# Retention in 64-token blocks packed into parts of the tensor array, and a gate product in four column groups

## The reference

```
def _retention_chunk(R, q, k, v):            # one block of L = CHUNK = 64 tokens
    s = einsum(q, k) * decay                  # causal, gamma ** (i - j)
    inner = einsum(s, v)
    cross = einsum(q, R) * q_dec              # gamma ** (i + 1)
    R_new = gamma ** L * R + einsum(k * k_dec, v)
    return R_new, inner + cross
r_out = _head_norm(r_out) * silu(rg)          # mean and variance over the 128 values of a head
```

## Time and profile before

| | us |
|---|---|
| median of 3 runs | 1840.75 (1840.66 to 1842.19) |
| the profiled execution, its own time | 1841.68 |
| its span, first to last instruction | 1839.8 |
| PE busy in the span | 1793.3 (97%) |
| DVE busy | 1158.7 (63%) |
| ACT busy | 578.5 (31%) |
| POOL busy | 115.7 (6%) |
| mean granted clock of PE | 0.991 |

### The profile page before, as it was taken

How to read it: one execution, slowest core, us unless ns; L and a number is a source line. 1 busy time by engine, 2 the same in 40 slices (tenths; PEclk the granted TensorE clock), 3 DMA queues, 4 the chain that set the end, 5 groups by cost and what they waited for, 6 DMA issues and landing times.

```text
span 1839.8 us, 31050 instructions
## 1 busy us (share of the span) xinstructions
PE 1793.3 (97%) x9636; PEld 1481.0 (80%) x9636; DVE 1158.7 (63%) x2588; ACT 578.5 (31%) x2032; POOL 115.7 (6%) x278
## 2 busy tenths in 40 slices
PE   5999999999999999999799999999999999999997
PEld 3787888888888888888678888888888888888886
DVE  3665566655666555665666766766666666666666
ACT  3321222212222212222334434434434344344342
POOL 1000000000000000010000000000000000000000
PEclk8999999999999999999899999999999999999999
DMA  9665555555555555554765565575565665655655
GB/s 374 201 169 172 134 147 148 136 137 139 127 151 147 125 142 134 138 141 133 199 172 157 155 191 147 155 187 143 165 180 147 172 170 147 182 163 146 191 141 143
DMA packets 488465, 296.64 MB, mean 161 GB/s; under 512 B 348626, under 2 KB 423570, under 8 KB 487396
## 3 DMA queue, kind: packets, MB, share of 16 engines
q1 hardware_dynamic: 488420, 296.08, 58.6%
HBM read 174.27 MB, written 121.71 MB: 161 GB/s over the span
## 4 chain that ended last, share of the span: by engine, by line
PE 92%; DVE 2%; issue 2%; DMA 2%; ACT 1%; SPq 1%; POOL 0%; POOLq 0%; DVEq 0%; ACTq 0%
PE bank L1305 80%; PE bank L1478 3%; PE bank L1501 2%; PE bank L1403 2%; PE bank L1389 2%; PE bank L1395 2%; PE bank L1401 2%; PE bank L1508 1%; DVE wl L321 1%; DMA stage<-in_w_out 1%; DMA xn_scratch<-xn 0%; PE bank L1458 0%; SPq L517 0%; DMA aqk_row<-aqk_scratch 0%; DMA xt<-in_x_prompt 0%
## 5 line engine op out<-in xcount | busy, mean ns | idle before, releaser
L1305 PE MATMUL bank<-wh,hh 128*128 128x512 f32 x1584 | 397.9, 393 | 5.9 <-DVE hh L1085 2.7
L1305 PE MATMUL bank<-wh,hl 128*128 128x512 f32 x1584 | 392.7, 390 | 0.0
L1305 PE MATMUL bank<-wl,hh 128*128 128x512 f32 x1584 | 391.8, 389 | 0.5 <-DVE wl L321 0.5
L1305 PEld LDWEIGHTS bank<-wh,hl 128*128 128x128 f32 x1584 | 297.8, 188 | 61.9
L1305 PEld LDWEIGHTS bank<-wl,hh 128*128 128x128 f32 x1584 | 297.2, 188 | 62.7 <-DVE wl L321 0.9
L1305 PEld LDWEIGHTS bank<-wh,hh 128*128 128x128 f32 x1584 | 292.9, 189 | 66.9 <-issue 7.3
L726 ACT ACTIVATE hf<-xn,tiny_a 128x128 f32<-128x128 f32 (+1 forms) x248 | 98.6, 480 | 373.8 <-DVE xn L919 373.8
L1228 DVE SCALAR_TENSOR_TENSOR a_gate<-a_gate,bank 128x128 f32<-128x128 f32 x132 | 29.1, 282 | 175.1 <-ACT a_gate L875 175.1
L1305 PE MATMUL bank<-wh,yh 128*128 128x512 f32 x528 | 132.1, 392 | 0.0
L1305 PE MATMUL bank<-wh,yl 128*128 128x512 f32 x528 | 130.8, 389 | 0.0
L1305 PE MATMUL bank<-wl,yh 128*128 128x512 f32 x528 | 130.8, 389 | 0.0
(11 more groups left out here) (167 smaller groups left out, 2434.5 us busy)
## 6 DMA issues: line engine op xcount, KB each, us to landing
xt<-in_x_prompt SPq DMA_DIRECT2D x64, 512.0 KB, 3.9
p_scratch<-p_in SPq DMA_DIRECT2D x264, 96.0 KB, 1.8
p_in<-p_scratch SPq DMA_DIRECT2D x66, 384.0 KB, 3.5
h_scratch<-hf SPq DMA_DIRECT2D x33, 512.0 KB, 2.9
hf<-h_scratch SPq DMA_DIRECT2D x33, 512.0 KB, 4.8
out<-xt SPq DMA_DIRECT2D x32, 512.0 KB, 4.5
xn_scratch<-xn SPq DMA_DIRECT2D x31, 512.0 KB, 2.9
xp<-xn_scratch SPq DMA_DIRECT2D x124, 128.0 KB, 3.1
```

Source lines behind the costliest of these rows:

```text
L1305: ins = mm(out, a[:, k, :], b[:, k, :], start=first and n == part[0] and k == chunks[0], stop=last and n == part[-1] and k == chunks[-1])
```

## The change

Retention is worked in two blocks of 64 tokens within a tile of 128. With c the block and h the head:

- scores: for each head two matmuls, 128 rows and 64 columns of the array, 64 moving columns; the decay table and the product on DVE halve to 256 columns.
- state: two updates for each head, one for each block, 64 rows and 128 columns of the array, 128 moving columns, into two banks (`upd_b`, `ky_b`). DVE makes the state after the first block in a new tile `state_mid` (4 instructions, `mid_done`), and the state after the second from that.
- queries times state and scores times values move into `weighted_values`, which stands behind group 1 instead of ahead of it. It waits for `gn_done` of the slot before, `mid_done` and `st_done`. Queries times state: 8 matmuls, 128 rows and 64 columns, 128 moving columns. Scores times values: 8 matmuls of 64 rows and 64 columns, 128 moving columns, the four of two heads in four quarters of the array. Outputs lie in two banks (`out_b` for heads 0 and 2, `xb0` for heads 1 and 3); for the odd heads the two blocks lie in swapped halves, so that the head norm takes two DVE instructions for each of them.
- the residual gate's product goes in four column groups of 256 moving columns instead of two of 512; its rows, loads and stores go in four pieces.
- in slot 32 the transposes of k wait for `state_done`; slot 0 of phase B uses another bank and `weigh` waits once for `gn_done`.

```diff
         state_s = sb("state_s", [P, COLS], F32, phase_a)
+        state_mid = sb("state_mid", [P, COLS], F32, phase_a)
         r_gate = sb("r_gate", [P, COLS], F32, phase_a)
         r_out = sb("r_out", [P, COLS], F32, phase_a)
-        decay = sb("decay", [P, COLS], F32, phase_a)
+        decay = sb("decay", [P, RH * HALF], F32, phase_a)
...
+        def row_block(h, c):
+
+            return HALF * ((c + h) % 2)
+
+        def out_of(h):
+
+            return (out_b, xb0)[h % 2][:, h * DK:(h + 1) * DK]
...
                 if back:
                     wait(dve, s_ready, t)
                     wait(dve, out_ready, t - 1)
-                    V.tensor_tensor(s_t[:, :], qs_b[:, :], decay[:, :], ALU.mult).then_inc(st_done, 1)
+                    V.tensor_tensor(s_t[:, 0:RH * HALF], qs_b[:, 0:RH * HALF], decay[:, :], ALU.mult).then_inc(st_done, 1)
                 if front:
                     wait(dve, za_ready, 4 * t + 1)
                     wait(dve, rope_loaded, 16 * (t + 1))
                     wait(dve, q_turned, t)
                     wait(dve, k_done, t)
                     rotate(t, za0, q_row, zq_read, q_mul, q_done)
+                if back:
+                    wait(dve, upd_ready, t)
+                    wait(dve, out_ready, t - 1)
+                    wait(dve, state_done, t - 1)
+                    st = state_s if static(i) and t - 1 == SAMPLE else state
+                    for h in range(RH):
+                        cols = slice(h * DK, (h + 1) * DK)
+                        last = V.scalar_tensor_tensor(state_mid[:, cols], st[:, cols], GAMMA[h] ** HALF, upd_b[:, cols],
+                                                      ALU.mult, ALU.add)
+                    last.then_inc(mid_done, 1)
...
-                        last = V.bn_stats(gn_stats[:, h, :], out_b[:, h * DK:(h + 1) * DK])
+                        last = V.bn_stats(gn_stats[:, h, :], out_of(h))
...
-                    wait(dve, upd_ready, t)
-                    st = state_s if static(i) and t - 1 == SAMPLE else state
+                    wait(dve, mid_done, t)
                     for h in range(RH):
                         cols = slice(h * DK, (h + 1) * DK)
-                        last = V.scalar_tensor_tensor(st[:, cols], st[:, cols], GAMMA[h] ** P, upd_b[:, cols], ALU.mult, ALU.add)
+                        last = V.scalar_tensor_tensor(st[:, cols], state_mid[:, cols], GAMMA[h] ** HALF, ky_b[:, cols],
+                                                      ALU.mult, ALU.add)
                     last.then_inc(state_done, 1)
...
-                        last = V.tensor_scalar(r_out[:, cols], out_b[:, cols], gn_mv[:, h, 0:1], gn_rstd[:, h:h + 1],
-                                               ALU.subtract, ALU.mult)
+                        if row_block(h, 0) == 0:
+                            last = V.tensor_scalar(r_out[:, cols], out_of(h), gn_mv[:, h, 0:1], gn_rstd[:, h:h + 1],
+                                                   ALU.subtract, ALU.mult)
+                        else:
+                            for c in range(2):
+                                at = slice(row_block(h, c), row_block(h, c) + HALF)
+                                last = V.tensor_scalar(r_out[c * HALF:(c + 1) * HALF, cols], out_of(h)[at, :], gn_mv[at, h, 0:1],
+                                                       gn_rstd[at, h:h + 1], ALU.subtract, ALU.mult)
...
+            def weighted_values(i, t):
+
+                wait(pe, gn_done, t - 1)
+                wait(pe, mid_done, t)
+                st = state_s if static(i) and t - 1 == SAMPLE else state
+                for h in range(RH):
+                    for c in range(2):
+                        cols, at = slice(h * DK, (h + 1) * DK), row_block(h, c)
+                        if h == RH - 1 and c == 1:
+                            wait(pe, st_done, t)
+                        mm(out_of(h)[at:at + HALF, :], q_t[:, h * DK + c * HALF:h * DK + (c + 1) * HALF],
+                           (st, state_mid)[c][:, cols], start=h < 2, stop=False, tile_position=(0, at))
+                for h in range(RH):
+                    for c in range(2):
+                        rows, cols = slice(c * HALF, (c + 1) * HALF), slice(h * DK, (h + 1) * DK)
+                        at = row_block(h, c)
+                        last = mm(out_of(h)[at:at + HALF, :], s_t[rows, h * HALF:(h + 1) * HALF], v_row[rows, cols],
+                                  start=False, stop=h >= 2, tile_position=(c * HALF, at))
+                last.then_inc(out_ready, 1)
...
-                        c = slice(h * DK, (h + 1) * DK)
-                        last = mm(qs_b[:, c], k_t[:, c], q_t[:, c], start=True, stop=True)
+                        for c in range(2):
+                            tok = slice(h * DK + c * HALF, h * DK + (c + 1) * HALF)
+                            last = mm(qs_b[c * HALF:(c + 1) * HALF, h * HALF:(h + 1) * HALF], k_t[:, tok], q_t[:, tok],
+                                      start=True, stop=True, tile_position=(0, c * HALF))
                     last.then_inc(s_ready, 1)
                     wait(pe, state_done, t - 1)
                     wait(pe, v_done, t)
                     for h in range(RH):
-                        c = slice(h * DK, (h + 1) * DK)
-                        last = mm(upd_b[:, c], k_row[:, c], v_dec[:, c], start=True, stop=True)
+                        for c in range(2):
+                            rows, cols = slice(c * HALF, (c + 1) * HALF), slice(h * DK, (h + 1) * DK)
+                            last = mm((upd_b, ky_b)[c][:, cols], k_row[rows, cols], v_dec[rows, cols], start=True, stop=True,
+                                      tile_position=(c * HALF, 0))
                     last.then_inc(upd_ready, 1)
-                    wait(pe, gn_done, t - 1)
-                    st = state_s if static(i) and t - 1 == SAMPLE else state
-                    for h in range(RH):
-                        c = slice(h * DK, (h + 1) * DK)
-                        mm(out_b[:, c], q_t[:, c], st[:, c], start=True, stop=False)
-                        wait(pe, st_done, t)
-                        last = mm(out_b[:, c], s_t[:, c], v_row[:, c], start=False, stop=True)
-                    last.then_inc(out_ready, 1)
+                    if not front:
+                        weighted_values(i, t)
...
                         dense(za1[:, :], h_hi, h_lo, group(1)).then_inc(za_ready, 1)
+                    if back:
+                        weighted_values(i, t)
...
+                        wait(pe, state_done, t)
...
-                            for j in range(2):
-                                last = mm(xb0[32 * j:32 * j + 2, :], c_silu[:, 2 * s + kk, :],
-                                          stage_view(n)[:, kk, j * COLS:(j + 1) * COLS], start=s == 0 and kk == 0,
+                            for j in range(4):
+                                last = mm(qs_b[32 * j:32 * j + 2, KV:2 * KV], c_silu[:, 2 * s + kk, :],
+                                          stage_view(n)[:, kk, j * KV:(j + 1) * KV], start=s == 0 and kk == 0,
                                           stop=s == 3 and kk == 1, tile_position=(0, 32 * j))
...
+                if static(i) and t == 0:
+                    pe.wait_ge(gn_done, SAMPLE + 1)
...
-    causal = (p[:, None] <= p[None, :]).astype(np.float64)
+    causal = (p[:, None] <= q[None, :]).astype(np.float64)
```

More of the change, by code:

```diff
@@ L80, in build_program @@
         ident = sb("ident", [P, P])
-        small = sb("small", [P, 64])
+        small = sb("small", [P, 32])
         neg_half = small[:, 0:8]
@@ L119, in build_program @@
         gn_mv = tiny_a[:, 28:36].rearrange("p (h s) -> p h s", h=RH)
[L120 to L125, removed]
+        c_in = tiny_a[:, 4:20].rearrange("p (c k) -> p c k", c=2)
+        c_th = tiny_a[:, 20:36].rearrange("p (c k) -> p c k", c=2)
+        c_silu = tiny_a[:, 36:52].rearrange("p (k c) -> p k c", c=2)
+        g_col = tiny_a[:, 52:60]
+        h_scale = tiny_a[:, 60:76].rearrange("p (k c) -> p k c", c=2)
+        h_shift = tiny_a[:, 76:92].rearrange("p (k c) -> p k c", c=2)
         mod_rows = s_t
@@ L201, in build_program @@
             sem(n) for n in ("gn_stat_done", "gn_mv_done", "gn_var_done", "gn_rstd_done", "gn_done", "yr_done"))
-        state_out, wide_set = sem("state_out"), sem("wide_set")
+        state_out, wide_set, mid_done = sem("state_out"), sem("wide_set"), sem("mid_done")
         rows_cleared, h_front, hi_front, lo_front = sem("rows_cleared"), sem("h_front"), sem("hi_front"), sem("lo_front")
@@ L385, in ag_bank @@
         def ag_bank(i, t):
-            return out0_b if static(i) and t == 0 else kg_b
+            return out1_b if static(i) and t == 0 else kg_b
         def static(i):
             return isinstance(i, int)
+        def row_block(h, c):
+            return HALF * ((c + h) % 2)
+        def out_of(h):
+            return (out_b, xb0)[h % 2][:, h * DK:(h + 1) * DK]
         def pe_turns(i, t):
@@ L487, in slot @@
```

(25 more changed lines are left out.)

2 lines of the change are left out of this document (1 added, 1 removed).

## The result

The changed kernel takes 1986.3 us (median of 4 runs, 1985.32 to 1987.65) against 1840.7, a ratio of 1.0787 with a 95% interval of 1.0774 to 1.0801. It is slower, as forecast, but by 146 us where 69 were forecast, and outside the range. The span of the profiled execution is 1985.6 us against 1839.8, 145.8 more; mean granted clock 0.972 against 0.991.

What follows compares the result with a forecast made beforehand. PE, busy for all 635.00 us of phase A's body, bounds the kernel. Profiled 1841.68 + 71.7 for slots 1 to 32 - 2.5 for the rest = 1910.9, 0.93 above the median, so 1910; range 1884 to 1945.

Steps and rivals of the forecast that it cites:

- gate and slot 33: Residual gate's product some 3.5 us shorter, once; slot 33 about 1 us longer through waits and head norm; together -2.5.
- The new wait: Before group 3 in every slot, PE stalls 2.22 us for DVE's read of k, which stands behind `out_ready`.
- Two instructions more at 0.34: DVE's head norm gets two more instructions, half the partitions taking the same time: 2 x 0.34 = 0.68 us.
- rival 2: The clock falls in PE's stall, one slow piece of 1.2 us in each slot: 39 us, 1949; chance 0.09.
- Nothing gained on PE: Retention on PE comes to 3.51 us a slot against 3.49, six changes of the array's division costing 0.84.
- The steps' sum: Retention's packed matmuls on PE, counted in steps without changes of the array's division, take 2.67 us a slot.
- Issue rate: PE's issue of the scores: 16 records in 0.45 us, 0.028 each, should be possible; 0.89 is their bound.
- Rival 3: `v_row`'s loop at group 0 binds too, practically a tie; 0.4 us a slot gives 1923; chance 0.15, inside the forecast.
- The cover for `state_mid`: DVE's 3.3 us from scores to statistics, `state_mid` included, hide under PE's 6.6 us through group 1; cost nothing.

Runs made afterwards that it cites:

- filling experiment: Changed kernel plus 18 wide matmuls of unused result ahead of group 3's wait for k's rotation, from tile 6 on: 1958.92 us, ratio 1.0635 to the kernel before.
- addresses-back kernel: Changed kernel with `tiny_a` allocated ahead of `stage23` and a pad in phase B, so stationary tiles start at multiples of 256 bytes again: 1967.99 us, ratio 1.0689.
- k first with addresses: Changed kernel with DVE's rotation of k ahead of its wait for `out_ready`, and stationary tiles back at multiples of 256 bytes: 1884.09 us, ratio 1.0227.

## Why the prediction was right and wrong

The sign, the mechanism and its place were right; the size was not. The 145.8 us between the spans come apart like this:

| | forecast | measured | from |
|---|---|---|---|
| PE waits for k's read | 32 x 2.22 = 71 | 88: 80.2 recorded, 32 x 0.29 for ends and restarts, less 1.5 for the one wait before | waits of the profile, starts in the timeline |
| lower clock behind the waits | 0 | 37 | 23 pieces at 1.6 us, the filling experiment |
| addresses of stationary tiles | not named | 15 | phase B, slots of the addresses-back kernel |
| PE's own work | 32 x 0.02 = 1 | 6 | slot of k first with addresses, 25.56 against 25.35 |
| gate and slot 33 | -2.5 | about 0, by the remainder only | |

- **The new wait**, the step that decided: shown. Putting k's rotation first takes 91 us away, putting the block back and `state_mid` forward 90. The term was mis-sized: 2.22 forecast, some 2.7 measured from start to start (8.34 - 5.58 = 2.76 in the slot shown), and a restart behind it. "Two instructions more at 0.34" failed: all six follow each other at 0.43, 2.58 instead of 2.04, and the chain is 0.68 longer than forecast; group 2, which takes 5.58 with its restart, hid 0.14 of it.
- **The clock** is the first step that failed. The text took rival 2's mechanism at 0.09, on the ground that most of a stretch around a 2.2 us stall stays busy. It fell behind two idle times in three, and without these 37 us the kernel would have come near 1949. The prediction had named a fall of the clock in the body as a sign that it is wrong. The rival's price, 39 us, came near 37 by luck: it took 32 pieces at 1.2 us, and there were 23 at 1.6. The row at hand, a fall behind a stretch broken by idle times, spoke for it, and the counterargument had no row of its own.
- **The addresses** were the second, a term put at nothing without a reason. `small` and `tiny_a` shrink in the edit, and the prediction passed over it; 15 us came of it. No row could have shown it beforehand, but the edit should have been named as an open cost.
- **Nothing gained on PE** held in its direction. The steps' sum was good: updates 1.09 and scores 0.62 (519.10 to 520.81 is 1.71, forecast 1.76 with the way back), the moved block 1.62 (forecast 1.61). The two retention stretches take 3.33 us, and the dense ones 25.56 - 3.33 = 22.23, which were 21.86 before. The rest of 0.2 above the kernel before is the forecast's 0.02 and six changes at 0.17 instead of 0.14.
- **Issue rate**: 16 records of the scores take 0.62 with the change included, 0.038 each. The Trainium skill, TensorE: Matmul & The Clock Gate, section "Wait — 56ns, not 53.3ns?", has 62 ns of the sequencer for each matmul when it is decoded in software, from which the prediction's estimate was 16 us more. Counted by records, as the estimate did, this burst is faster than that, and the 16 us did not come. Whether the two records of a float32 matmul count once, and which way of decoding is in use, no run shows.
- **Rival 3**, `v_row`'s loop, was there, one step behind: with the first wait gone it showed at 0.8 us a slot, and behind it k's reload.
- **The cover for `state_mid`** held: it ends over 3 us ahead of the moved block (522.16 + 0.88 against 526.50).

## What to carry to other kernels

When a block is moved later on the engine that sets the pace, follow what another engine has queued behind its signal, in that engine's own order; here a saving of nothing on PE was paid with 88 us of waiting, and reordering DVE's list took most of it back. An idle time of PE was priced twice in this kernel, once as time and once as the lower clock behind it. And a change in the size of one small tile moves the addresses of all that follow: keep large stationary operands where they were, or pad.

## What was not expected of the hardware

- Wide float32r matmuls whose stationary tile starts 128 bytes off a multiple of 256 take 232 ns instead of 227 start to start, in phase A and B alike; tiles that did not move keep 227. Only this one offset was tried, so which multiple matters is open, and whether the weight load or something else is behind it.
- Behind idle times of 2.4 to 2.6 us, one a slot, the granted clock fell to its lower level for 3.4 us in 17 of the 26 slots of tiles 6 to 31. Behind 1.2 to 1.4 us it did not fall in the 24 slots of tiles 6 to 29, and behind the single one of 1.93 us in the same run it did. What decides in the slots between is open.
- A 128x128 tensor_scalar out of PSUM, four in a row, follows at 0.34 us; in a row with 64x128 ones at 0.43, whole height or half. The change of bank from head to head is not the reason: with the blocks in the same halves the banks still change, and the four take 1.36 us. Whether it is the change of height or that the half-height ones read one half and write the other was not separated.
